# VectorE's steps ahead of its low parts in the three mixers of a fused two-block transformer kernel

## What is computed

```python
# first block's mixer
q, k, v, q_idx, k_idx, w_idx, x_lru, g_lru = split(modulate(rmsnorm(x)) @ w_in)
score = sum_h(relu(q_idx @ k_idx.T / 8) * w_idx);  keep the 64 best admissible keys of each token
attn  = softmax(q @ k.T / 8 + bias over the kept keys) @ v
lru   = linear_scan(exp(log_a), mult * sigmoid(..) * conv4(x_lru)) * gelu(g_lru)
x = x + m[5] * rmsnorm(concat(rmsnorm(attn), rmsnorm(lru)) @ w_out)
# hybrid mixer, twice
hq, hf, hi, hg, aq, ak, av, sz, sxbc, sdt = split(rms_norm(x) @ w_in)
mix = concat(hgrn2(hq, hf, hi, hg), dilated_attention(aq, ak, av), mamba2(sz, sxbc, sdt))
x = x + mix @ w_out
```

## Time and profile before

| | us |
|---|---|
| median of 3 runs | 2553.1 |
| lowest, highest | 2552.1, 2553.4 |
| the profiled execution | 2550.3 |
| its span (first to last instruction) | 2548.5 |
| TensorE busy | 2443.1 |
| VectorE busy | 1689.7 |
| ScalarE busy | 1204.1 |
| GpSimd busy | 716.1 |

### The profile page before, as it was taken

One profiled execution on the slowest core, in us unless ns is written; L12 is line 12 of the kernel. 1 busy time (PEld: TensorE's weight loads), 2 busy tenths in 40 slices (PEclk: granted clock), 3 DMA queues, 4 the chain that ended last, 5 costly groups with the idle time before them and its releaser, 6 DMA issues.

```text
span 2548.5 us, 40330 instructions
## 1 busy us (share of the span) xinstructions
PE 2443.1 (96%) x16347; PEld 2234.9 (88%) x16347; DVE 1689.7 (66%) x3111; ACT 1204.1 (47%) x1827; POOL 716.1 (28%) x333
## 2 busy tenths in 40 slices
PE   4999989999999999999999999999999999999999
PEld 3997978988889999999888888789999999988887
DVE  6887766546565788899544445564868899744444
ACT  4434655446554444443444445554444443444443
POOL 3111001112025671000344443114664000244443
PEclk9999999999999999999999999999999999999999
DMA  7987534664345554444665655335455444566554
GB/s 280 337 301 291 178 124 166 205 200 163 100 148 169 171 169 158 140 140 138 197 193 193 196 191 195 106 118 176 166 174 162 139 140 141 178 194 194 194 191 165
DMA packets 126588, 457.45 MB, mean 179 GB/s; under 512 B 13973, under 2 KB 16961, under 8 KB 125634
## 3 DMA queue, kind: packets, MB, share of 16 engines
q1 hardware_dynamic: 121442, 441.52, 52.2%
q10 hardware_dynamic: 4048, 8.91, 1.0%
q0 software_dynamic: 912, 4.42, 0.5%
HBM read 451.62 MB, written 5.93 MB: 180 GB/s over the span
## 4 chain that ended last, share of the span: by engine, by line
PE 78%; DVE 7%; ACT 1%; issue 1%; POOL 0%; ACTq 0%; DVEq 0%
PE bank L607 23%; PE bank L609 23%; PE bank L608 23%; PE bank L1170 4%; DVE sb L1846 1%; DVE sb L2608 1%; ACT sb L1213 1%; DVE sb L2604 1%; PE bank L1146 1%; PE bank L1098 0%; PE bank L955 0%; PE bank L622 0%; PE bank L816 0%; DVE sb L2611 0%; DVE sb L2451 0%
## 5 line engine op out<-in xcount | busy, mean ns | idle before, releaser
L607 PE MATMUL bank<-sb,sb 128*128 128x256 f32 (+1 forms) x4744 | 1521.1, 321 | 50.7 <-DVE sb L1846 28.7
L609 PE MATMUL bank<-sb,sb 128*128 128x256 f32 (+1 forms) x4744 | 1494.8, 315 | 0.0
L608 PE MATMUL bank<-sb,sb 128*128 128x256 f32 (+1 forms) x4744 | 1494.7, 315 | 0.0
L1213 ACT ACTIVATE sb<-sb 128x1024 fp32r<-128x1024 f32 x765 | 806.3, 1058 | 1073.9 <-PE bank L609 1068.8
L1846 DVE TENSOR_TENSOR sb<-sb,sb 128x1024 fp32r<-128x1024 f32 x509 | 633.2, 1245 | 605.5 <-ACT sb L1213 604.2
L2716 POOL TENSOR_TENSOR sb<-sb,sb 128x1024 fp32r<-128x1024 f32 x256 | 650.2, 2542 | 1328.1 <-ACT sb L1213 1324.1
L607 PEld LDWEIGHTS bank<-sb,sb 128*128 128x128 f32 x4744 | 908.6, 192 | 120.4 <-issue 34.0
L609 PEld LDWEIGHTS bank<-sb,sb 128*128 128x128 f32 x4744 | 908.2, 191 | 56.0
L608 PEld LDWEIGHTS bank<-sb,sb 128*128 128x128 f32 x4744 | 909.2, 192 | 54.9 <-issue 1.0
L2680 DVE TENSOR_TENSOR sb<-sb,sb 128x1024 fp32r<-128x1024 f32 x64 | 159.9, 2498 | 149.9 <-ACT sb L1802 149.9
L2643 DVE TENSOR_SCALAR sb<-sb,sb 128x128 f32<-128x128 f32 x512 | 150.6, 357 | 0.0
(11 more groups left out here) (274 smaller groups left out, 1248.8 us busy)
## 6 DMA issues: line engine op xcount, KB each, us to landing
sb<-in_peer_down_dram SPq DMA_DIRECT2D x256, 512.0 KB, 3.3
sb<-in_peer_up_dram SPq DMA_DIRECT2D x256, 512.0 KB, 3.3
sb<-in_w_ada_dram SPq DMA_DIRECT2D x72, 512.0 KB, 6.2
sb<-in_hyb_in_dram SPq DMA_DIRECT2D x56, 512.0 KB, 3.3
sb<-in_ffn_gate_dram SPq DMA_DIRECT2D x44, 512.0 KB, 4.3
sb<-in_ffn_up_dram SPq DMA_DIRECT2D x44, 512.0 KB, 4.6
sb<-in_ffn_down_dram SPq DMA_DIRECT2D x44, 512.0 KB, 4.3
sb<-in_mix_in_dram SPq DMA_DIRECT2D x25, 512.0 KB, 3.4
```

Of the source, the lines that this page charges most:

```text
L607: e.matmul(out, a[0], b[0], start=start, stop=False)
L608: e.matmul(out, a[0], b[1], start=False, stop=False)
L609: return e.matmul(out, a[1], b[0], start=False, stop=stop)
L1213: self.e.activation(rr(M.hi[k % NSPLIT]), M.raw[k % NRAW], AF.Copy).then_inc(*self.S.tick("hi", k))
```

## The change

VectorE sets `ahead_first` to False ahead of slot 0 (first mixer) or slot 2 (hybrid) and back to True behind the last slot. The other four engines keep their order.

```diff
--- before.py
+++ after.py
@@ -2259,6 +2259,7 @@
         self.features()
         self.tasks = {"select": self.select(), "rows": self.rows(),
                       "recurrence": self.recurrence(), "attention": self.mix_attention()}
+        self.ahead_first = False
         self.linear(7)
         wi = M.tiny("mix1", "wi", 16)
         self.wait_ge("wi_copy")
@@ -2284,6 +2285,7 @@
 
         self.part = part
         self.contract(8)
+        self.ahead_first = True
         self.gated_residual()
 
 
```

## The result

| | before, us | after, us |
|---|---|---|
| median | 2552.8 (4 runs) | 2530.2 (4 runs) |
| lowest, highest | 2552.1, 2553.4 | 2528.0, 2531.5 |
| profiled execution | 2550.3 | 2531.5 |
| its span | 2548.5 | 2529.7 |

The ratio is 0.990, with a 95% interval of 0.9885 to 0.9915: 22.6 us faster by the medians. The forecast was 2528 us, with a range of 2521 to 2543 that was to hold the time 8 times in 10.

A forecast was written before the change was run, and what follows sets the result against it. TensorE, busy 2443.1 of 2548.5 us, was taken as the bound, waiting for VectorE's steps. Gains of 15.6 + 6.9 + 2.5 = 25.0 us from median 2553.1 gave 2528 us, range 2521 to 2543, 8 times in 10.

The forecast's parts named there:

- six waits: Both hybrid mixers: TensorE's waits for VectorE's steps go, 15.6 us in all, bounds nothing and 15.6.
- the half-clock stretches: Hybrid mixers: slow-clock stretches behind the waits go with them, 6.9 us gained, bounds 0 and 8.5.
- The cost of the low parts: Hybrid mixers: later low parts still arrive in time, cost 0, upper bound 2.4 us, one low part per layer.
- The rival in which a wait takes the place of each: Hybrid mixers: the put cannot run earlier, the 15.6 us stay; 2548 to 2555 us, chance 0.05.
- the slower one: Hybrid mixers, slot 21 and after: TensorE waits for late low parts; 2563 us, chance 0.05.
- The own range of the forecast: 2521 to 2534 us: first mixer 4.8 better, or 2.4 of late low parts and half the clock's term.
- The rival in which the falls stay or move: Waits go but half-clock stretches stay or fall elsewhere: 2537.5 us, chance 0.15.
- stretches of the same number: Sign of being wrong: as many half-clock stretches after the change as before.
- The term: First mixer: waits together 0 (bounds 3.5 lost, 4.8 gained), clock 2.5 us gained at tile 25.
- Low part 12: First mixer, slot 9's step ahead of it: a new TensorE wait of 2.4 us near 298.
- Low part 13: First mixer, behind slot 10's step: 1.2 us more wait for TensorE.
- The sum: Whole kernel: 15.6 + 6.9 + 2.5 = 25.0 us gained, forecast 2528 us against the median 2553.1.

The follow-up runs named there:

- the second execution: Profiled execution of the whole change run again, nothing altered, beside a kernel before of 2553.6 us: 2527.5 us; its four runs had median 2530.8, ratio 0.9908.
- the early slots alone: Against the kernel before, steps first only in slots 2 to 16 of both hybrid mixers: 2541.3 us, ratio 0.9944.
- the kernel without slots 28 and 29: The whole change, but slots 28 and 29 of both hybrid mixers in the old order: 2537.5 us, ratio 0.9918 to before.
- the second occasion: Later runs together on the first chip, including the whole change unaltered: before 2553.6 us, whole change 2530.8 us, ratio 0.9908.
- the kernel without slot 14: The whole change, but slot 14 of both hybrid mixers in the old order: 2539.3 us, ratio 0.9927 to before.
- Five slots of the first mixer: Whole change in the hybrid mixers, first mixer steps first only in slots 20 to 24: 2524.0 us, ratio 0.9864 to before; again 2525.2, 0.9887.

## Why the prediction was right, and where its sizes were off

**The waits of the hybrid mixers, and the clock there.** The prediction took 15.6 us for six waits and 5.3 + 1.6 for the half-clock stretches, 22.5 in all. The mixers became 8.9 and 13.4 us shorter, 22.4 together, and 24.4 in the second execution. The mechanism is the one forecast; that the first of these figures agrees to 0.1 us is luck. All idle of TensorE in the two mixers, from their first transposition to that of the next stage, fell by 15.1 us (14.6 in the second execution), against the 15.6 forecast for the six waits; the work itself became 7.3 us (9.8) shorter, against 6.9 for the clock. All six waits fell as it said, L1098's to 0.2 us each instead of to nothing. Waits of 0.8 us for L2490 are left in both layers, of which the sum had nothing. The cost of the low parts was put at 0, with an upper bound of 2.4 us; there is no TensorE wait for L1846 in either hybrid mixer. The rival in which a wait takes the place of each, and the slower one, are excluded by that and by the idle. The own range of the forecast, 2521 to 2534, has a slip at its lower end: 4.8 us better in the first mixer gives 2523, and 2521 needs the clock's upper bound as well.

**The clock** was the term in doubt. The trace of before had two equal waits with different outcomes, and the early slots alone and the kernel without slots 28 and 29 show the same again (gaps of 1.62 and 1.64 both followed by a fall; gaps of 2.06, one with and one without). No run here shows why. The Trainium skill's "TensorE: Matmul & The Clock Gate", section "What's actually happening", has the gate run free of the kernel. The runs are in line with it in so far as a stretch of 10.2 us came in one layer, and that of the other shrank from 10.2 to 6.8, with the waits ahead of L1098 unchanged. That the stretches stood behind waits was nevertheless the better guide for this change: with no wait above 0.8 us left inside the hybrid mixers behind their first tiles, no fall is left there either.

The rival in which the falls stay or move came true in part, though its time of 2537.5 did not. Outside the three mixers, their first tiles counted as outside, the half-clock stretches grew from 17 us to 39 in this execution and to 27 in the second. Over the whole span they are 44 us before, 45 in this execution (2531.5 us) and 31 in the second (2527.5). One of the forecast's signs of being wrong, stretches of the same number, is thus met by the profiled execution: there were ten before and twelve are there now, though eight in the second one. The net worth of the clock is better seen over several executions. On the second occasion the mean granted clock was 0.987 to 0.990 in the seven runs of before and 0.991 to 0.994 in the four of the whole change. An estimate from these means, span times the missing share, is a loss of 29 us before and 21 after: about 8 us of gain for the clock, against 9.4 forecast in all three mixers.

**The first mixer.** The term was 2.5 us, with waits even and the clock's 2.5 as gain, and it measured 1.6 and 3.2. The waits came nearly as worked out. Low part 12 was to come 2.4 us late near 298; it was 2.17 late at 302.8. Without the wait the tile would have started at 300.7, and the mixer began 2.5 us later than before, so this is the place forecast. Low part 13 was to cost 1.2 more. In this trace it does not; tile 12 ran at half clock (the first of these windows), which gives VectorE the time:

```profile
303.10:306.50 3.40, 3.40 (x18) 3.40 (x18) 3.22 (x10) 0.00 (x0) 0.00 (x0) 0.51 0.46 154
378.20:381.60 3.40, 3.40 (x10) 2.64 (x9) 0.33 (x1) 0.00 (x0) 0.00 (x0) 0.50 0.47 160
```

In the kernel without slot 14, whose first mixer is the changed one, the wait for low part 12 is also 2.17 us but is followed by no fall, and there low part 13 costs TensorE 0.69:

```profile
307.32 0.36 PE L610 MATMUL bank<-sb,sb 128*128 128x256 f32 x1 [0.69 <-DVE sb L1854]
```

That mixer is 1.0 us shorter than that of the profiled one. So the term whose working was off, though its size came out within the scatter, is the clock's in the first mixer, taken as a plain gain of 2.5 us. The fall of 6.8 us behind the biases went, and so did one of 3.4 behind the gate's wait, but two of 3.4 came for them in this execution, behind the new wait of 2.17 us and behind L1948's, which had grown to 1.99 and of which the prediction had nothing; in the second execution only the first of the two came, and the mixer is 1.6 us shorter. The waits together came out as taken, nearly even: those for the gate and the biases shrank by 2.6 and 3.3 us (the latter to 1.2 instead of the 2.5 forecast), and paid for four on low parts (2.17, 1.22, 0.77, 0.39) and 0.7 more at L1948. VectorE's group of low parts in 294 to 353 us shows the idle that went into it, 1.0 us where the earlier trace rows has 4.8:

```profile
L1846 DVE TENSOR_TENSOR sb<-sb,sb 128x1024 fp32r<-128x1024 f32 x14 | 18.1, 1294 | 1.0 <-ACT sb L1213 1.0
```

**The sum.** 25.0 us of gain were forecast, and 22.6 measured by the medians (22.8 on the second occasion). The mixers gave 24.0 and 27.6; the rest is given back in unchanged stages. The forecast had taken the profiled execution of before as 2.8 us quicker than the median, and this fits: its first feed-forward layer had no half-clock stretch. The 2.2 us by which the median missed are within what the runs of one kernel scatter.

## What to carry to other kernels

In this kernel, on an engine that works in order, a piece of work that nobody needs soon and that itself waits (here a low part, waiting for its high part, with tiles of slack) cost more in front of a step than its length: one low part of 1.22 us in slot 14 brought back a wait of 2.5 us and a slow stretch. Put first what another engine waits for next. But choose by slot: where the engine had idle the exchange was free, where it was full for tens of microseconds the work that was put off made a wait of its own, and where the step's own operand was barely there the exchange brought nothing. Five slots of the first mixer made it 7.0 us shorter where all of them made it 1.6 to 3.2.

## What the runs showed of the hardware that was not expected

The length of a gap does not decide whether the granted clock falls behind it: gaps of 2.06 us ahead of the same 36 multiplications ended in 4.20 us of work in one layer and 7.91 in the other. The same happens between two executions of one kernel: with the whole change the wait of 2.0 us for L1948 in the first mixer is followed by a half-clock stretch in the first execution (above, at 378.2) and by none in the second:

```profile
378.70 0.50 PE L607 MATMUL bank<-sb,sb 128*128 128x512 f32 x1 [1.99 <-DVE sb L1948]
```

```profile
378.00:384.00 6.00, 5.30 (x23) 4.37 (x24) 2.97 (x6) 1.93 (x3) 0.00 (x0) 1.00 0.53 173
```

With the early slots of the hybrid mixers alone a stretch of 10.2 us stood on a stage that had none before; a profile of one execution can thus show a slow stretch that the kernel does not always have.

A second surprise is in a lookup layer, which the change does not touch. TensorE's waits for VectorE's low parts from 900 to 1000 us of the span, first in the profiled execution of after, then in the second one of the same kernel:

```profile
PE bank L607 <- DVE sb L1846: 4.2, 1, 4.2
```

```profile
PE bank L607 <- DVE sb L1846: 2.4, 1, 2.4
PE bank L607 <- POOL sb L2720: 1.3, 1, 1.3
```

One kernel has there once a single wait of 4.2 us, with a half-clock stretch behind it, and once two of 2.4 and 1.3 as before the change; the layer is 820.1 and 818.5 us long. The single wait of 4.2 us stands in 8 of the 28 lookup layers of the fourteen traces, none of them in the one of before. What decides between the two was not found.
